# Second FFN's upward product: seven products of 256 tokens for eight, its weight sums made by adding DMAs in DRAM

## The reference

```python
def modulate(x, g, shift, scale):
    return rmsnorm(x, g) * (1.0 + scale[:, None, :]) + shift[:, None, :]

def swiglu(h, w_up, w_down):
    gate, up = jnp.split(h @ w_up, 2, axis=-1)
    return (jax.nn.silu(gate) * up) @ w_down
...
        h = modulate(x, g_ffn2[l], shift[:, 2], scale[:, 2])
        x = x + 0.5 * gate[:, 2][:, None, :] * swiglu(h, w_ffn2_up[l], w_ffn2_down[l])
    return rmsnorm(x, g_final)
```

## Time and profile before

| | |
|---|---|
| median of 3 runs | 1125.18 us (1124.54 to 1125.28) |
| profiled execution, its own time | 1125.46 us |
| its span | 1123.7 us |
| PE busy | 1101.7 us, 98% |
| DVE busy | 597.4 us, 53% |
| ACT busy | 445.2 us, 40% |
| POOL busy | 71.7 us, 6% |
| mean DMA rate | 119 GB/s |

### The profile page before, as it was taken

The page is one execution under the profiler, slowest core; times in us unless marked ns, Lnnn a source line. Parts: engine busy times, 40 slices in busy tenths (PEclk is TensorE's granted clock), DMA queues, the critical chain, the costliest instruction groups (busy, mean ns, idle before and its releaser), DMA issues.

```text
span 1123.7 us, 14298 instructions
## 1 busy us (share of the span) xinstructions
PE 1101.7 (98%) x5142; PEld 882.4 (79%) x5142; DVE 597.4 (53%) x829; ACT 445.2 (40%) x693; POOL 71.7 (6%) x68
## 2 busy tenths in 40 slices
PE   8999999999999999999999999999999999999997
PEld 5788888888788878888778778778888888878876
DVE  3745555555554536977876775663333333434343
ACT  5523222222222225867885765352222222221322
POOL 1000000000000001000000000000000000234440
PEclk9999999999999999999999999999999999999999
DMA  9755667556573732332222212323333333232221
GB/s 339 226 150 149 192 200 201 153 168 187 147 230 94 218 97 66 87 83 56 76 67 57 66 48 57 92 65 90 93 93 94 93 93 93 74 103 94 85 94 76
DMA packets 169687, 133.32 MB, mean 119 GB/s; under 512 B 5436, under 2 KB 150956, under 8 KB 169644
## 3 DMA queue, kind: packets, MB, share of 16 engines
q1 hardware_dynamic: 168704, 130.60, 39.8%
q0 software_dynamic: 768, 2.10, 0.8%
q10 hardware_dynamic: 172, 0.06, 0.0%
HBM read 128.54 MB, written 2.10 MB: 116 GB/s over the span
## 4 chain that ended last, share of the span: by engine, by line
PE 89%; DVE 3%; ACT 3%; DMA 3%; issue 1%; SPq 0%; DVEq 0%; POOL 0%; ACTq 0%
PE bank L711 27%; PE bank L713 27%; PE bank L712 27%; PE bank L1029 1%; PE bank L731 1%; PE bank L1001 1%; PE bank L977 1%; DMA w_raw<-in_w_ffn_down_dram 1%; DVE w_lo L1488 1%; ACT w_hi L1124 1%; PE bank L978 1%; DMA x_nat<-in_x_dram 1%; DMA k_hh_b<-k_hh_b 0%; PE bank L1062 0%; PE bank L757 0%
## 5 line engine op out<-in xcount | busy, mean ns | idle before, releaser
L1488 DVE TENSOR_TENSOR w_lo<-w_raw,w_hi 128x1024 fp32r<-128x1024 f32 x163 | 216.8, 1332 | 384.5 <-ACT w_hi L1124 383.9
L711 PE MATMUL bank<-h_hi,w_hi 128*128 128x512 f32 x864 | 348.9, 404 | 0.3 <-DVE h_lo L1561 0.2
L713 PE MATMUL bank<-h_hi,w_lo 128*128 128x512 f32 x864 | 342.2, 396 | 0.0
L712 PE MATMUL bank<-h_lo,w_hi 128*128 128x512 f32 x864 | 342.1, 396 | 0.0
L1124 ACT ACTIVATE w_hi<-w_raw 128x1024 fp32r<-128x1024 f32 x163 | 172.3, 1058 | 424.3 <-PE bank L713 394.9
L711 PEld LDWEIGHTS bank<-h_hi,w_hi 128*128 128x128 f32 x864 | 162.8, 188 | 42.7 <-issue 4.2
L712 PEld LDWEIGHTS bank<-h_lo,w_hi 128*128 128x128 f32 x864 | 162.8, 188 | 40.7 <-issue 2.9
L713 PEld LDWEIGHTS bank<-h_hi,w_lo 128*128 128x128 f32 x864 | 162.7, 188 | 39.4
L612 POOL TENSOR_TENSOR w_raw<-w_raw,gate_row 128x1024 f32<-128x1024 f32 (+1 forms) x24 | 54.9, 2286 | 377.6 <-DMA w_raw<-in_w_ffn_down_dram 377.2
L711 PE MATMUL bank<-w_hi,hid_hi 128*128 128x512 f32 x176 | 70.4, 400 | 3.1 <-DVE w_lo L1488 3.1
L711 PE MATMUL bank<-hid_hi,w_hi 128*128 128x512 f32 x176 | 70.1, 398 | 2.2 <-DVE w_lo L1488 2.2
(11 more groups left out here) (215 smaller groups left out, 1330.0 us busy)
## 6 DMA issues: line engine op xcount, KB each, us to landing
w_raw<-in_w_ffn_up_dram SPq DMA_DIRECT2D x88, 512.0 KB, 4.9
ada_w<-in_w_ada_dram SPq DMA_DIRECT2D x56, 512.0 KB, 3.9
w_raw<-in_w_ffn_down_dram SPq DMA_DIRECT2D x36, 512.0 KB, 4.5
w_raw<-in_w_in_dram SPq DMA_DIRECT2D x28, 512.0 KB, 3.9
ada_first<-in_w_ada_dram SPq DMA_DIRECT2D x16, 512.0 KB, 10.8
w_raw<-in_w_out_dram SPq DMA_DIRECT2D x8, 512.0 KB, 3.9
w_raw<-in_w_ffn_down_dram SPq DMA_DIRECT2D x8, 384.0 KB, 4.8
x_nat<-in_x_dram SPq DMA_DIRECT2D x4, 512.0 KB, 5.3
```

The costliest lines, as they stand in the source:

```text
L711: mm(dst, wh, xh, start=start, stop=False, skip_group_check=skip)
L712: mm(dst, wh, xl, start=False, stop=False, skip_group_check=skip)
L713: return mm(dst, wl, xh, start=False, stop=stop, skip_group_check=skip)
L1488: v.tensor_tensor(w_lo[:, s, :], w_raw[:, r, :], w_hi[:, s, :].bitcast(F32), ALU.subtract)\
```

## The change

The product of weights (2 x 2 blocks: gate and up, upper and lower 512 rows) and activations (2 x 2 blocks: upper and lower 512 features, left and right 256 tokens) is done from the third pair on (`SEVEN0 = 2`, 20 pairs) with seven block products for eight.

- **Weight sums.** Four sums of weight blocks are made for the 2560 columns of those pairs in a new DRAM tensor `w_sums`: S1 = up_a + up_b, S3 = gate_a + up_a, S2 = gate_a + S1, S4 = gate_b + S2. POOL issues 32 pieces of 128 rows by 2560 columns (1.31 MB each): 16 plain copies DRAM to DRAM and 16 that add what they carry to what stands in DRAM. At most two are in flight. Eight copies are issued in the first FFN's down stage, the other 24 in groups of four ahead of `repeat_k(1)` to `repeat_k(6)`.
- **Activation sums.** After the norm ACT keeps the full h (`keep_h`), and DVE and ACT make four combinations t1 to t4 with high and low part.
- **Products.** A pair loads 3.5 tiles in four loads (gate; S2 and S1; S3 and S4; lower half of up) for 2, into three sets of raw buffers. PE runs 7 products of 4 chunks by 3 matmuls of 128x256, 84 matmuls for 48. ACT copies two partial sums out of the banks, DVE adds them up (7 operations of 128x256 a pair).
- **Hidden.** The product silu x up stays in float32 (`hid`), and all 22 chunks are split at the end of the stage. Splits of the down tiles now cover only the columns in use.

The pair loop is written out. Core of the diff:

```diff
+SEVEN0 = 2
+T_DOWN2 = T_UP2 + 2 * SEVEN0 + 4 * (FC - SEVEN0)
...
+            def one_piece(dst, src, add):
+                n = pieces[0]
+                if n >= 2:
+                    pool.wait_ge(sums_made[n % 2], 16 * (n // 2))
+                dst, src = (a.rearrange("p (c n) -> p c n", c=2) for a in (dst, src))
+                if add:
+                    ins = g.dma_start(dst, src, accum_op=ALU.add, max_dma_last_dim=2 * width)
+                else:
+                    ins = g.dma_start(dst, src)
+                ins.then_inc(sums_made[n % 2], 16)
+                pieces[0] += 1
+            for r in range(4):
+                pool.wait_ge(w_used, T_DOWN1 + 6 * r + 1)
+                one_piece(sums_rows(S1, r), pieces_rows(up_a, r), False)
+                one_piece(sums_rows(S3, r), pieces_rows(gate_a, r), False)
...
             for j in range(1, JOBS):
+                if j == 1:
+                    for r in range(4):
+                        one_piece(sums_rows(S1, r), pieces_rows(up_b, r), True)
+                elif j == 2:
+                    for r in range(4):
+                        one_piece(sums_rows(S3, r), pieces_rows(up_a, r), True)
+                elif j == 3:
+                    for r in range(4):
+                        one_piece(sums_rows(S2, r), pieces_rows(gate_a, r), False)
+                elif j == 4:
+                    for r in range(4):
+                        one_piece(sums_rows(S2, r), sums_rows(S1, r), True)
+                elif j == 5:
+                    for r in range(4):
+                        one_piece(sums_rows(S4, r), pieces_rows(gate_b, r), False)
+                elif j == 6:
+                    for r in range(4):
+                        one_piece(sums_rows(S4, r), sums_rows(S2, r), True)
                 repeat_k(j)
...
+            def product(dst, f, q, part, xh, xl, start):
+                hi, lo = up_hi[f % 2][q], up_lo[(f - SEVEN0) % 3][q]
+                for k in range(4):
+                    cols = slice((4 * part + k) * P, (4 * part + k + 1) * P)
+                    last = three(dst, hi[:, cols], lo[:, cols], xh[:, k, :], xl[:, k, :],
+                                 start and k == 0, k == 3, skip=True)
+                return last
...
+                product(first, f, 0, 0, *b11, True).then_inc(part_done, 1)
...
+                product(sixth, f, 1, 0, *c_t2, True).then_inc(part_done, 1)
...
+                product(fifth, f, 1, 1, *c_t1, True).then_inc(w_used, 1)
+                pe.wait_ge(p1_done, n + 1)
+                product(first, f, 0, 1, *b21, False).then_inc(w_used, 1)
...
+                pe.wait_ge(u_done, n + 1)
+                product(sixth, f, 2, 0, *c_t3, False).then_inc(part_done, 1)
+                pe.wait_ge(p5_done, n + 1)
+                product(fifth, f, 2, 1, *b22, False).then_inc(w_used, 1)
...
+                pe.wait_ge(c22_part, n + 1)
+                product(sixth, f, 3, 0, *c_t4, False).then_inc(w_used, 1)
...
+            for f in range(SEVEN0, FC - 1):
+                seven_low(f + 1, 0)
+                sixth_plus_first(f)
+                seven_low(f + 1, 1)
+                seven_low(f + 1, 2)
+                right_up(f)
+                seven_low(f + 1, 3)
+                right_gate(f)
+                left_up(f)
+                both_hidden(f)
```

More of the change, by code:

```diff
@@ L532, in z_read, with uses, parts, half_of @@
             return (d_ready, unit + 1) if unit < 5 * SBJ else (max_done, unit - 5 * SBJ + 1)
+        def uses(f, q):
+            return T_UP2 + 4 * (f - 1) + (2, 1, 3, 4)[q]
+        def parts(f, n):
+            return 3 * (f - SEVEN0) + n
+        def half_of(buf, n):
+            return buf[:, n * HALF:(n + 1) * HALF]
+        kept_g1, kept_g2 = half_of(tmp_a[:, 0, :], 0), half_of(tmp_a[:, 0, :], 1)
+        kept_c12, kept_c21 = half_of(tmp_a[:, 1, :], 0), half_of(tmp_a[:, 1, :], 1)
+        def bank_of(f, what):
+            return {"first": (0, 1), "sixth": (6, 3), "fifth": (7, 2)}[what][f % 2]
+        def sum_of(f, what):
+            return half_of(bank[bank_of(f, what)], 0)
+        def hid2_hi(c):
+            return hid2_hi_a[:, c, :] if c < 4 else hid2_hi_b[:, c - 4, :]
         def tile_used(t):
@@ new lines, in keep_first, with keep_fifth @@
+            def keep_first(f):
+                n = f - SEVEN0
+                act.wait_ge(part_done, parts(f, 1))
+                if n >= 2:
+                    act.wait_ge(c21_done, n - 1)
+                a(kept_p1[f % 2], sum_of(f, "first"), ACT.Copy).then_inc(p1_done, 1)
+            def keep_fifth(f):
+                n = f - SEVEN0
+                act.wait_ge(w_used, uses(f, 1))
+                if n >= 2:
+                    act.wait_ge(c22_done, n - 1)
+                a(kept_p5[f % 2], sum_of(f, "fifth"), ACT.Copy).then_inc(p5_done, 1)
@@ L1439, in _ @@
-            nc.scalar.preload_act_table_set("silu_and_others")
-            split_hi(T_UP2 + 2 * SPLIT, used=T_UP2)
-            split_hi(T_UP2 + 2 * SPLIT + 1, used=T_UP2 + 1)
-            for j in range(2):
+                if h:
+                    act.wait_ge(w_lo_done, T_UP2 + RAW)
+                a(gate_row[h][:, 0, :], bank[6 + h][:], ACT.Copy).then_inc(row_copied, 1)
+            for k in range(KC - 2, KC):
+                keep_h(k)
+            nc.scalar.preload_act_table_set("silu_and_others")
@@ L1443, in _ @@
+            seven_high(SEVEN0, 0)
+            combo_high(2, t2, 1, -1.0)
+            combo_high(1, t1, 0, 1.0)
+            seven_high(SEVEN0, 1)
+            for j in range(SEVEN0):
                 act.wait_ge(w_used, T_UP2 + 2 * j + 1)
                 a(tmp_a[:, j, :], bank[j][:], ACT.Silu).then_inc(silu_done, 1)
[L1445 to L1449, removed]
@@ L1453, in square_out @@
+            f = FC - 1
+            hidden2_high(0)
+            keep_first(f)
+            hidden2_high(1)
+            hidden2_high(2)
+            keep_fifth(f)
+            hidden2_high(3)
+            for chunk in range(4, 6):
+                hidden2_high(chunk)
+            silu_left(f)
+            split_down(T_DOWN2)
+            silu_right(f)
+            split_down(T_DOWN2 + 1)
+            for chunk in range(6, FC):
+                hidden2_high(chunk)
             def square_out(half, tb):
```

380 lines of the change are left out of this document (313 added, 67 removed).

## The result

The changed kernel takes 1129.71 us (median of 12 runs, 1126.68 to 1135.7) against 1125.1 for the one before (12 runs): a ratio of 1.0042, 95% interval 1.0023 to 1.006. It is slower by 0.4%, where 1112 and faster was predicted. The profiled execution is the fastest of the twelve, 1126.68 us with a span of 1124.9, only 1.2 us longer than before, where the medians are 4.6 apart.

A forecast was written before the change was run, and what follows sets the result against it. The upward product was taken as bound by PE's own pace. From 1125.5 us, minus 23.6, plus 2.4, minus 2.0 and plus 10 for the adding pieces gave 1112.3, stated as 1112; range 1099 to 1150.

The forecast's parts named there:

- The eight plain copies in the first down stage have it easy: First FFN's down stage: engines idle 56 us, eight pieces take 8 x 3.2 to 8 x 5.6 us, so no cost.
- PE's pace: Second FFN's up stage, twenty pairs: 84 half-width matmuls a pair at 0.1196 us, 200.9 for 224.5 us, minus 23.6 us.
- Steady state: Within the twenty pairs: ACT, DVE, bank hand-overs and loads keep up with PE, taken as 0.
- Passage to the third pair: Start of the third pair: PE waits for DVE's `kept_u`, plus 2.4 us, range 0 to 5.
- Passage to the down stage: Into the second down stage: 0 to 1.5 us new wait against narrower splits, minus 2.0 us, between -3 and +2.
- The adding pieces in the mixer: Mixer: job 2's key copies behind eight adding pieces come between just in time and 19.5 us late; plus 10 us.
- The price of 6.4 us a piece: Adding pieces: both operands read at the output stores' rate, 407 GB/s at full share; 11.2 us was the upper bound.
- Rival 2: Mixer: key copies far behind the adding pieces, at 9 us a piece job 2's 40 us late, 1149 us; chance 0.31.
- listed signs of being wrong: Pieces over 9 us apart, mixer weight loads late enough that ACT waits, or a matmul step over 0.125 us.
- Weight loads four tiles ahead can give way: Mixer: weight loads can yield to pieces part of the time but must be served, hence the middle, plus 10 us.
- Hidden pieces: Rival: pieces make key copies late by at most 4 us, total 1102 to 1106 us; chance 0.27.
- The seams of short products: Rival, twenty pairs: 140 product seams at 0.085 us cost 12 us, total 1124 us, scheme doesn't pay; chance 0.10.

The follow-up runs named there:

- Experiments two: Changed kernel with only the eight plain copies kept; the mixer's 24 pieces are left out: 1118.95 us, ratio 0.9958.
- three: Changed kernel with the eight plain copies moved behind later tiles of a turn of twelve, one at a time: 1114.1 us, ratio 0.9894.
- six: Kernel of experiment five with the eight copies put back near their old places, one at a time: 1111.1 us, ratio 0.9877.
- seven: Kernel of experiment five with the eight copies left at the new places but issued two at once: 1105.33 us, ratio 0.9834.
- Experiment eight: Kernel without pieces, with POOL's gating cut to 8 of 512 columns: single run, span 1095.8 us against 1100.3 without this edit.
- nine: Changed kernel with DVE summing the right half of up ahead of the low parts in each pair: 1134.54 us, ratio 1.0105.
- ten: Kernel of experiment five, with DVE's right-half sums earlier and the third down tile split after the fifteenth hidden chunk: 1101.66 us, ratio 0.9789.
- experiment four: Changed kernel with the mixer's adding pieces made plain copies, so sums are not formed: 1120.1 us, ratio 0.9952.
- experiments five: Kernel of experiment three with the mixer's 24 pieces spread over the windows between key copies: 1103.25 us, ratio 0.981.

## Why the prediction was wrong

**The step that failed** is "The eight plain copies in the first down stage have it easy". It compared 26 to 45 us of pieces with 56 us in which the engines are idle. That is an average over 128 us, and the price of a piece in it was right: the two pieces at 294 us took 0.409 of 20 us, 4.1 us each, and at 0.70 over 143 us the engines still are far from full. What counts is how long before its use each tile is issued. Where SP is one tile ahead, PE wants a tile 5.8 us after its issue (297.7 to 303.5), and two pieces in front of it make landing alone 10.5 us. Experiments two, three, six and seven show it: the same bytes in pairs cost 17 us at the old places and 3 at the new ones (with the spread pieces of the mixer in it), singly 9 and 1. Part of the price is not the wait: of the 15.1 us in the first down stage, 8.4 + 5.4 - 2.6 (the gap that stood at 303.5 before) = 11.2 are longer gaps, and the rest is the lower clock at their ends. SP's order of loads could be read before; I did not look at it. The trace before also had its one wait of that stage, 2.2 us, at this very tile: issued at 298.26 and used at 306.17, it had no slack at all, whatever the mean share of the DMA engines.

**PE's pace** was right: 0.1191 us a matmul for 0.1196. Without its two waits (4.4 us) the stretch is 202.1 us for 200.9, and some 1.5 of that is the half clock at the end of the second. **Steady state** at no cost was right too: PE waits for nothing there.

**Passage to the third pair:** 2.4 us were predicted and 0.4 of wait measured. The size was off, within its range of 0 to 5.

**Passage to the down stage:** the stage itself gained 2.9 us for 2.0. But a wait of 4.0 us, with 3.4 us of half clock at its end, fell in the last pair, in front of it. I had seen that POOL's gating may slow DVE and counted it only after PE's last product, where it has room; it begins when the down tiles land, at 977, during the pair, where DVE owes PE a sum. Experiment eight shows it, and in nine and ten, with DVE's sum ahead of the low parts, the wait is below 1 us.

**The adding pieces in the mixer:** 10 predicted, 8.0 in the profiled execution; the two other traces with the same order there have more (335.2 us in experiment three, 332.0 in nine, for 318.3 before), so the sign holds, and the size is uncertain by several us. The price of 6.4 us a piece stands: from 459 to 510 us POOL's queue took 0.883 of 51 us, 45.0, for 9.06 MB, that is four key copies of 0.13 MB at 0.56 us (their 2.10 MB were 0.8% of 1123.7 us before, for sixteen) and 6.5 pieces, at (45.0 - 2.2) / 6.5 = 6.6 us. The estimate of 5.3 us by the Trainium skill (Collectives: The Full Stack, The bandwidth ceiling) was low: the trace agrees with two reads for each result (an adding packet holds an engine as long as a plain one of twice its bytes), but a plain packet moved 10240 B in 387 ns, 26 GB/s an engine. Rival 2's estimates of 6.1 us for a plain piece and 9.2 for an adding one were high: the same sum over experiment four's trace, 0.740 of 51 us less the key copies for 9.5 plain pieces, gives 3.7.

The way to the 8.0 us was only in part the forecast one. The expected waits of 5 us in jobs 1 and 2 were 3.6 and 0.9, and the clock, for which the sum had no term, was at its lower level from 491.3 to 498.1 us, across the end of the first. One of the listed signs of being wrong came true as well: ACT did wait for weight loads, 9.8 us in all. "Weight loads four tiles ahead can give way" held for PE in the profiled execution, and failed in experiment three's, where such a load cost PE 4.3 us.

**The rivals.** The measured 1129.7 lies in the stated range of 1099 to 1150, but by luck: it is in the part that was held open for rival 2, whose late key copies did not cost that. Hidden pieces (1102 to 1106) was not what this order gives, but what experiments five and seven reach with the same pieces. Slower by key copies far behind gave the right sign for a wrong reason: key copies cost 8 and not 40 us. The seams of short products did not show. No rival held the weight tiles of the first down stage.

**What stays open.** The change's runs spread over 9 us, those of the kernel without pieces over 1.5, and its median is 3 us above the one execution that was traced. That the mixer is what varies fits experiments three and nine, but is not shown, since only one execution of each was traced. How much of the mixer's loss is late key copies and how much late weight loads was not measured apart either. How the engines share their time between POOL's queue and the weight loads, packet by packet, was not measured apart.

## What to carry to other kernels

Before a bulk transfer is put into a stage with idle DMA engines, list the issue times of that stage's loads and how long after its issue each is wanted; the transfer goes where loads run several tiles ahead, and on an in-order queue it goes behind the small copies that others wait for, or so far ahead of them that it has landed. A mean DMA share says nothing about this; a short wait that already stands at a place does. Fewer matmuls in front of DVE's deadlines need a second look at every place where another engine slows DVE, above all at stage borders.

## What the runs showed of the hardware

- Wait and clock. Around the end of a wait of 8.0 us the granted clock was at 1.2 GHz for 10.2 us, around that of 5.0 us for 3.4, of 4.0 us (`kept_c`) for 3.4 and of 3.6 us for the keys of job 1 for 6.8. PE worked in the last 5.6, 3.3, 2.9 and 5.6 us of them at half its pace, so by an estimate from these rows the clock cost 1.5 to 2.8 us on top of each wait. The kernel before, with a gap of 2.6 us at 303.5, kept the full clock there.
- A plain piece and an adding one. Adding pieces followed one another on POOL's queue every 7.1 to 7.8 us (470.33, 477.43, 484.67, 491.88, 499.65), beside the mixer's loads. With the pieces as plain copies all queues together moved 318 GB/s from 459 to 510 us at a share of 0.98, with adding ones 222 at 1.05.
- DVE beside POOL. A float32 subtraction of 128x512 with two inputs in SBUF took 2.7 and 1.7 us beside POOL's multiplications and 0.69 without, an addition with one input in a bank 0.42 either way.
